# A hybrid decoder layer on one core: the delta rule's scan in one PSUM bank, and four edits beside it

## Time and profile before

| | us |
|---|---|
| median of 3 runs (lowest, highest) | 1223.63 (1221.22, 1224.39) |
| profiled execution, its own time | 1222.85 |
| its span, first to last instruction | 1221.1 |
| PE busy / PEld busy | 1151.6 / 936.6 |
| DVE / ACT / POOL busy | 801.5 / 558.4 / 483.8 |
| mean granted clock of PE | 0.991 |

### The profile page before, as it was taken

The page is one execution under the profiler, slowest core; times in us unless marked ns, Lnnn a source line. Parts: engine busy times, 40 slices in busy tenths (PEclk is TensorE's granted clock), DMA queues, the critical chain, the costliest instruction groups (busy, mean ns, idle before and its releaser), DMA issues.

```text
span 1221.1 us, 22297 instructions
## 1 busy us (share of the span) xinstructions
PE 1151.6 (94%) x9202; PEld 936.6 (77%) x9202; DVE 801.5 (66%) x1093; ACT 558.4 (46%) x1005; POOL 483.8 (40%) x420
## 2 busy tenths in 40 slices
PE   5999999889998989999998999999999999999996
PEld 4778879877777776767666778888888888888784
DVE  5798977457788888888874854333333333777974
ACT  6544233346554445454555654333333334446442
POOL 2476346212022021220213024554445554875972
PEclk9999999999999999999998999999999999999998
DMA  7345121400000000000105443222222221553561
GB/s 247 85 114 178 54 50 46 89 22 22 2 21 21 2 22 2 21 2 3 36 10 182 144 152 101 70 69 74 82 69 70 69 77 62 211 185 121 186 227 69
DMA packets 104076, 99.82 MB, mean 82 GB/s; under 512 B 15412, under 2 KB 89384, under 8 KB 103976
## 3 DMA queue, kind: packets, MB, share of 16 engines
q1 hardware_dynamic: 102536, 93.15, 25.1%
q10 hardware_dynamic: 1440, 5.24, 1.1%
HBM read 85.24 MB, written 13.11 MB: 81 GB/s over the span
## 4 chain that ended last, share of the span: by engine, by line
PE 69%; DVE 19%; ACT 5%; issue 4%; DMA 2%; SPq 1%; POOL 0%; DVEq 0%; ACTq 0%; POOLq 0%
PE psum L1694 25%; PE psum L1990 12%; PE psum L2531 6%; PE psum L1340 5%; PE psum L2571 4%; DVE arena L2414 3%; PE psum L1521 3%; PE psum L1587 3%; DVE pt_q L1237 2%; PE psum L1497 2%; PE psum L1537 1%; DVE arena L1218 1%; ACT pt_p L1017 1%; DVE ap_q L1866 1%; PE psum L1333 1%
## 5 line engine op out<-in xcount | busy, mean ns | idle before, releaser
L1694 PE MATMUL psum<-h_p,up_p 128*128 128x512 f32 x704 | 221.0, 390 | 0.7 <-DVE h_q L1683 0.5
L1694 PE MATMUL psum<-h_q,up_q 128*128 128x512 f32 x704 | 220.7, 389 | 0.0
L1760 POOL TENSOR_TENSOR up_q<-arena,up_p 128x1024 fp32r<-128x1024 f32 x44 | 105.9, 2406 | 212.3 <-ACT up_p L1756 212.3
L1811 DVE SCALAR_TENSOR_TENSOR arena<-psum,arena 128x1023 f32<-128x1023 f32 x44 | 56.4, 1283 | 196.1 <-ACT arena L1780 196.1
L1694 PEld LDWEIGHTS psum<-h_p,up_p 128*128 128x128 f32 x704 | 132.1, 188 | 28.9 <-DVE h_q L1683 1.0
L1694 PEld LDWEIGHTS psum<-h_q,up_q 128*128 128x128 f32 x704 | 132.2, 188 | 27.3
L1780 ACT ACTIVATE arena<-psum,arena 128x1024 f32<-128x1024 f32 x44 | 49.1, 1117 | 199.0 <-PE psum L1694 199.0
L1850 POOL TENSOR_TENSOR dn_q<-arena,dn_p 128x1024 fp32r<-128x1024 f32 x44 | 114.5, 2617 | 44.1 <-ACT dn_p L1846 44.1
L1866 DVE SCALAR_TENSOR_TENSOR ap_q<-ap_p,arena 128x512 fp32r<-128x512 f32 x44 | 108.9, 2499 | 29.3 <-ACT ap_p L1862 29.3
L1990 PE MATMUL psum<-dn_p,ap_p 128*128 128x512 f32 x352 | 110.7, 396 | 6.1 <-DVE ap_q L1866 6.1
L1340 PE MATMUL psum<-arena 64*64 64x64 f32 x3072 | 112.6, 223 | 3.5 <-DVE arena L1109 1.6
(11 more groups left out here) (299 smaller groups left out, 2327.0 us busy)
## 6 DMA issues: line engine op xcount, KB each, us to landing
arena<-in_ffn_w_up SPq DMA_DIRECT2D x44, 512.0 KB, 3.8
arena<-in_ffn_w_down SPq DMA_DIRECT2D x44, 512.0 KB, 3.5
arena<-in_w_in SPq DMA_DIRECT2D x20, 512.0 KB, 4.0
arena<-in_x SPq DMA_DIRECT2D x16, 512.0 KB, 5.0
qkv_mid<-arena ACTq DMA_DIRECT2D x9, 512.0 KB
...
```

The source lines that it names most:

```text
L1694: ins = pe.matmul(up_ps[j % 2][:, g, h * 512:(h + 1) * 512], w[:, k], x[:, k, h * 512:(h + 1) * 512], start=k == 0 and x is h2_p, stop=Tru ...
L1760: pool.tensor_tensor(up_q[up_slot(u)], up_st[up_slot(u)], up_p[up_slot(u)], ALU.subtract).then_inc(late("up_lo")[0], 1)
L1811: v.scalar_tensor_tensor(out=y[:, 1:S], in0=ps[:, 0:S - 1], scalar=tap(1, u), in1=y[:, 1:S], op0=ALU.mult, op1=ALU.add).then_inc(late("up_ ...
```

## The change

Five edits. (a) The scan: every step of both chunks uses bank 2. For a chunk the steps are now `B1`, `B3`, `C1`, `B2`: o is completed at once, ACT copies it out to `on` and squares it (two instructions for 64 rows each time, 16 times), and only then `B2` overwrites the place. `C1n` becomes one operation on `on` in SBUF rather than two that read PSUM. (b) `NT` uses bank 3 for every second step from the sixth on, with semaphores of its own, so that two turned blocks can stand at a time. (c) `ORDER` is another string throughout. (d) The down stage: from kk = 3 on DVE forms `dn_q`, just ahead of `ap_q`, and makes all residual additions; POOL has nothing left there. The two loads of norm gains ahead of the output stage are issued earlier and no longer one after the other. (e) The first two units are done by blocks of 256 tokens, the first after the transposes of tile 2.

```diff
 def gdn_scan(t):
-    return [("B1", t, 0), ("B2", t, 0), ("B1", t, 1), ("B2", t, 1), ("B3", t), ("C1", t), ("C1r", t), ("C1s", t), ("C1n", t), ("C2", t)]
+    return [(s, t, c) for c in range(2) for s in ("B1", "B3", "C1", "B2")] + [("C1r", t), ("C1s", t), ("C1n", t), ("C2", t)]
...
-    "gsgggiisgiisgssssssgstssgssssgsstssggsvvstsssgsssrvgvsgoisgosossggsstssgsvvtggvvstssgosssvvstggosssg"
...
+    "gsgggiisggiiisgsssgsssssgtsssgvsvssssggtssssggstssgvsrsgvsgosoogstssvggvvsvsgsstsstsggsosssvvvgstsgt"
...
+        nsa_nt = [s for s in MIX if s[0] == "NT"]
+        nsa_p3 = nsa_nt[5::2]
+        nsa_pt = [s for s in MIX if s[0] in ("Nq", "Nc2", "Nidx", "Nb", "No") or s in nsa_nt and s not in nsa_p3]
         def pt_use(step):
             return nsa_pt.index(step)
-        nsa_nt = [s for s in MIX if s[0] == "NT"]
-
-
-        nt_alt = [s for s in nsa_nt[-NT:] if nsa_pt[pt_use(s) - 1] in nsa_nt[-NT:]][::2]
-
-        def nt_bank(step):
-            return 4 if step in nt_alt else 6
+        def nt_at(step):
+            if step in nsa_p3:
+                return 3, sem("n_p3m"), sem("n_p3"), nsa_p3.index(step)
+            return 6, sem("n_ptm"), sem("n_pt"), pt_use(step)
+        def nt_turned(eng, step):
+            _, turned, _, u = nt_at(step)
+            eng.wait_ge(turned, u + 1)
...
+            def C1(t, c):
+                act.wait_ge(sem("b_o"), 2 * t + c + 1)
                 if t:
                     act.wait_ge(sem("c_ss"), t)
-                for rows, bank in O_AT:
-                    act.activation(flat(sq2)[rows], psum[rows, bank, 0:GDIM], ACT.Square).then_inc(sem("c_sq"), 1)
+                    act.wait_ge(sem("c_tp"), t)
+                rows = O_AT[c]
+                act.activation(flat(on)[rows], psum[rows, 2, 0:GDIM], ACT.Copy).then_inc(sem("c_oc"), 1)
+                act.activation(flat(sq2)[rows], psum[rows, 2, 0:GDIM], ACT.Square).then_inc(sem("c_sq"), 1)
...
+                v.tensor_tensor(flat(vn)[rows], psum[rows, 2, 0:GDIM], flat(uu[t % 2])[rows], ALU.add).then_inc(sem("b_vn"), 1)
...
-                for rows, bank in O_AT:
-                    v.tensor_tensor(on[rows], psum[rows, bank, 0:GDIM].rearrange("p (h d) -> p h d", h=GH), bc(rs2[rows], 2, HD), ALU.mult)\
-                        .then_inc(sem("c_on"), 1)
+                v.wait_ge(sem("c_oc"), 2 * t + 2)
+                v.tensor_tensor(on, on, bc(rs2, 2, HD), ALU.mult).then_inc(sem("c_on"), 1)
...
 def B2(t, c):
                 rows = (LO, HI)[c]
+                pe.wait_ge(sem("c_oc"), 2 * t + c + 1)
+                pe.wait_ge(sem("c_sq"), 2 * t + c + 1)
+                for h in range(GH):
+                    ins = pe.matmul(psum[(LO, HI)[h % 2], 2, h // 2 * CH:(h // 2 + 1) * CH], kdec[t % 2][rows, h], vn[rows, h],
+                                    start=h < 2, stop=True, skip_group_check=True)
+                ins.then_inc(sem("b_dm"), 1)
+
+            def B3(t, c):
+                rows = (LO, HI)[c]
+                pe.wait_ge(sem("g_QTc"), t + 1)
                 pe.wait_ge(sem("b_vn"), 2 * t + c + 1)
                 for h in range(GH):
-                    out_rows, bank = D_AT[c][h % 2]
-                    ins = pe.matmul(psum[out_rows, bank, h // 2 * CH:(h // 2 + 1) * CH], kdec[t % 2][rows, h], vn[rows, h],
-                                    start=h < 2, stop=True, skip_group_check=True)
-                ins.then_inc(sem("b_dm"), 1)
-
-            def B3(t):
-                pe.wait_ge(sem("g_QTc"), t + 1)
-                pe.wait_ge(sem("b_S"), 4 * t + 4)
-                for h in range(GH):
-                    for rows, (out_rows, bank) in zip((LO, HI), O_AT):
-                        ins = pe.matmul(psum[out_rows, bank, h * CH:(h + 1) * CH], QTc[t % 2][rows, h], vn[rows, h], start=False, stop=True,
-                                        skip_group_check=True)
+                    ins = pe.matmul(psum[O_AT[c], 2, h * CH:(h + 1) * CH], QTc[t % 2][rows, h], vn[rows, h], start=False, stop=True,
+                                    skip_group_check=True)
                 ins.then_inc(sem("b_o"), 1)
 
             def C2(t):
-                pe.wait_ge(sem("c_on"), 2 * t + 2)
+                pe.wait_ge(sem("c_on"), t + 1)
...
                 step = ("NT", t, kind, kv, b)
-                before = nsa_pt[pt_use(step) - 1] if pt_use(step) else None
-                if step in nt_alt:
-                    pe.wait_ge(sem("n_exp"), 2 * NH * NT)
-                if before in nsa_nt[-NT:] and nt_bank(before) != nt_bank(step):
-                    pe.wait_ge(sem("n_pt"), pt_use(step) - 1)
-                else:
-                    pt_free(step)
+                bank, turned, done, n = nt_at(step)
+                if step == nsa_p3[0]:
+                    pe.wait_ge(sem("kc_mul"), 4)
+                    pe.wait_ge(sem("vc_out"), 6)
+                if n:
+                    pe.wait_ge(done, n)
                 u = s_use(t, kind, GRP * kv)
                 pe.wait_ge(sem("n_exp"), u + GRP)
                 k0, _ = key_blocks(t, kind)
                 for g in range(GRP):
-                    ins = pe.transpose(psum[:, nt_bank(step), g * P:(g + 1) * P], probs(u + g)[:, (b - k0) * P:(b - k0 + 1) * P], ident)
-                ins.then_inc(sem("n_ptm"), 1)
+                    ins = pe.transpose(psum[:, bank, g * P:(g + 1) * P], probs(u + g)[:, (b - k0) * P:(b - k0 + 1) * P], ident)
+                ins.then_inc(turned, 1)
 
             def NV(t, kind, kv, b):
-                pe.wait_ge(sem("n_pt"), pt_use(("NT", t, kind, kv, b)) + 1)
+                _, _, done, u = nt_at(("NT", t, kind, kv, b))
+                pe.wait_ge(done, u + 1)
...
             sp.wait_ge(sem("n_sm"), 2 * NH * NT)
+            sp.dma_start(gpost_mix, a["norm_mix_post"][0].partition_broadcast(P)).then_inc(sem("gpost_in"), 16)
+            sp.dma_start(gffn, a["norm_ffn_pre"][0].partition_broadcast(P)).then_inc(sem("gpost_in"), 16)
             sp.wait_ge(sem("n_ptm"), pt_use(("No", NT - 1)) + 1)
             sp.wait_ge(sem("b_S"), 4 * NT)
             sp.wait_ge(sem("c_m"), 2 * NT)
             for t in range(3):
                 sp.dma_start(xr[t], x_d[0, t * P:(t + 1) * P, :]).then_inc(late(f"xr_in{t}")[0], 16)
-            sp.dma_start(gpost_mix, a["norm_mix_post"][0].partition_broadcast(P)).then_inc(sem("gpost_in"), 16)
-            sp.wait_ge(sem("gpost_in"), 16)
-            sp.dma_start(gffn, a["norm_ffn_pre"][0].partition_broadcast(P)).then_inc(sem("gpost_in"), 16)
...
-        def dn_split_lo(pool, kk):
-            pool.wait_ge(*late("dn_hi", kk + 1))
-            pool.tensor_tensor(dn_q[kk % 4], dn_st[kk % 4], dn_p[kk % 4], ALU.subtract).then_inc(late("dn_lo")[0], 1)
+        def dn_split_lo(eng, kk):
+            eng.wait_ge(*late("dn_hi", kk + 1))
+            eng.tensor_tensor(dn_q[kk % 4], dn_st[kk % 4], dn_p[kk % 4], ALU.subtract).then_inc(late("dn_lo")[0] if kk < 3 else sem("dn_lv"), 1)
+        def dn_ready(eng, kk):
+            eng.wait_ge(*late("dn_lo", kk + 1)) if kk < 3 else eng.wait_ge(sem("dn_lv"), kk - 2)
...
                 if kk >= 4:
-                    sp.wait_ge(*late("dn_lo", kk - 3))
+                    dn_ready(sp, kk - 4)
...
-            for kk in range(3, DN):
-                dn_split_lo(pool, kk)
-                if kk in (NF + 3, NF + 5):
-                    add(kk - NF - 3)
-            for t in range(HT, NT, 2):
-                add(t)
...
             for kk in range(2, DN):
                 if kk == NF + 2:
                     for t in range(HT):
                         finish(t)
+                if kk > 2:
+                    dn_split_lo(v, kk)
                 act_split_lo(v, kk)
 
-                if kk in (NF + 4, NF + 5):
-                    add(2 * (kk - NF - 4) + 1)
+                if NF + 4 <= kk < NF + 4 + HT:
+                    add(kk - NF - 4)
...
-            def unit(i, halves=(0, 1), ks=range(KD)):
+            def unit(i, blocks=((0, 512), (512, 1024))):
...
-                for k in ks:
+                for k in range(KD):
                     for w, x in ((p, h_p), (q, h_q)):
-                        for h in halves:
-                            ins = pe.matmul(cm_ps[i % 2][:, h * 512:(h + 1) * 512], w[:, k], x[:, k, h * 512:(h + 1) * 512],
+                        for c0, c1 in blocks:
+                            ins = pe.matmul(cm_ps[i % 2][:, c0:c1], w[:, k], x[:, k, c0:c1],
                                             start=k == 0 and x is h_p, stop=True, skip_group_check=True)
-                if 1 in halves:
+                if c1 == S:
...
-                if t >= NT // 2:
-                    pe.wait_ge(sem("h_lo"), NT // 2)
-                    if t == 6:
+                for i, b in {2: ((0, 0),), 4: ((1, 0),), 5: ((0, 1),), 6: ((1, 1),), 7: ((0, 2), (1, 2))}.get(t, ()):
+                    pe.wait_ge(sem("h_lo"), 2 * b + 2)
+                    if (i, b) == (1, 0):
                         pe.wait_ge(sem("pcol_ready"), 3)
```

(6 more changed lines are left out.)

72 lines of the change are left out of this document (28 added, 44 removed).

## The result

| | before | after |
|---|---|---|
| median of 4 runs each (lowest, highest), us | 1223.86 (1221.22, 1224.39) | 1206.23 (1204.77, 1206.69) |
| span of the profiled execution, us | 1221.1 | 1202.5 |
| PE / DVE / ACT / POOL busy, us | 1151.6 / 801.5 / 558.4 / 483.8 | 1143.9 / 765.5 / 559.7 / 365.9 |
| mean granted clock of PE | 0.991 | 0.989 |

The ratio is 0.9858, 95% interval 0.9841 to 0.9875: 17.6 us faster, where 9.5 were forecast. The time is inside the range and outside the likeliest case (1209 to 1218); it is that of rival 1.

The account below looks back on a forecast made before the run. PE was taken to bound the kernel (69% of the chain), edits elsewhere paying only where PE waits. Down -2.8, output -1.2, first -0.5, mixer -5.0 sum to -9.5: 1213.4 from 1222.85, 1214.1 us as median; range 1204 to 1227.

Parts of the forecast that it names:

- rival 1: Mixer: the order frees more, turning in pairs takes all 16.5 us of load waits; mixer some -14, time 1205; chance 0.17.
- Down stage, -2.8: Down stage: PE's first wait goes (-1.9), second shortens (-0.9), clock dip of some 2.4 us stays; bounds -5.2 and 0.
- First stage, -0.5: Front: last `h_q` about 0.5 us earlier, so DVE's chain from the rope tables gains 0.5; bounds -1.5 and +1.5.
- Rival 3: First stage: PE's longer idle time near 74 us drops the clock, costing up to 2.4 us: 1216.5; chance 0.08.
- (i): Mixer: second place for turned probabilities removes PE's 18 waits for `pt_q`, -7.4 us; bounds 0 and -16.5.
- (ii): Mixer: `C1n` as 8 operations instead of 16 saves DVE 4.4 us; a third taken, -1.4; bounds 0 and -4.4.
- (iv): Mixer: `B2` waits for copy and square, about 1.1 us per chunk, mostly hidden: +1; bounds 0 and +17.6.
- rival 4: Mixer: slower, `B2` behind ACT's copy and square costs PE about 2 us per exposed chunk; ten give 1233; chance 0.20.
- (iii): Mixer: ACT gains 16 copies, 7.7 us of work on an engine with free time: +0.8; bounds 0 and +7.7.
- (v) the end, +2: Mixer's end: fewer steps ahead of the last `C2`, a new copy of 0.48, output product at half clock; bounds 0 and +4.
- The rest of the new order: Mixer: remaining effect of the new order, not priceable from rows, taken as nought with 8 us to either side.
- Rival 2: Mixer stands still, waits for `pt_q` move to `NV`; only -4.5 is left, 1219.1 us; chance 0.17.

Follow-up runs that it names:

- b_down: Kernel before with only the down stage's second parts and residual additions moved from POOL to DVE, gain loads left as they were: 1218.66 us, ratio 0.9957.
- b_first: Kernel before with only the first units of products done in blocks of two tiles: 1221.67 us, ratio 0.9994.
- b_b3seq: Kernel before with `B3`'s two loops exchanged, six products of the lower rows, then six of the upper, instead of by turns: 1226.69 us, ratio 1.0023.
- b_scan: Kernel before with only the scan in bank 2, its copies and one `C1n`; old order except the scan's own steps, placed anew: 1232.94 us, ratio 1.0078.
- a_oldorder: Changed kernel with the old written order, only the scan's own steps placed anew, second bank in use: 1220.84 us, ratio 0.9987 to the kernel before.
- a_split: Changed kernel with 36 of 37 side-by-side pairs of `NT` steps taken apart in the order: 1214.64 us, ratio 0.9929 to the kernel before.

## Why the prediction was right or wrong

**Down stage, -2.8.** Mechanism right, size short: -3.8 in the changed kernel, -5.4 alone (-4.6 by the medians). `ap_q` has its 0.684 in the median and `dn_q` 1.225 on DVE, both as priced; the first wait is gone, the second is 3.16 (3.3 forecast). The mis-sized term is the dip of the clock, "I leave in place", which measured 0.8 us less in the changed kernel and 2.4 less in b_down, where it did not come; the bound of -5.2 had allowed for that. Why the clock fell in four of the five traces with this wait and not in the fifth stays open.

**Output stage, -1.2.** Mechanism right in the traces, size not measurable in the medians. DVE's wait for the gain went, and with it PE's wait of 1.2 us ahead of the first turned tile, as said. The stage is 3.1 us shorter, since the new order also took the last `NV` and the wait ahead of the last `No` out of it, a term that the prediction does not have.

**First stage, -0.5.** Not shown (b_first), and the place was wrong: the step "PE's idle time there grows to some 2.7 us" put it at unit 6, near 74 us, where PE did not wait at all. It came ahead of unit 2, since ScalarE's copy of unit 0 was late. Rival 3's fall of the clock came with it (pairs at 1.05 us), but there DVE sets the pace and it cost nothing.

**Mixer, -5.0.** Measured -10.8, and the sum of the terms hid two steps that failed, in opposite directions.
- *(i) second bank, -7.4:* -8.6 under the old order by the traces, 7.5 at most by the medians. The size is right. The mechanism is right only in part: the waits ahead of the transposes went, but most of that idle time came back at other steps (2.3 us less in all), and 6.3 us of the gain is busy time. That the sizes agree is in part luck.
- *(ii) to (iv), the scan, together +0.4:* +9.2 in the trace (434.4 - 425.2), +9.7 in the medians. The step that failed is one that the prediction does not have: it costed what `B3` waits for and not how its products follow each other on PE. The lost alternation costs 3 us by the medians, 4.6 by the traces (b_b3seq). `B2` waits for ACT by 1.5 us, near the +1 of (iv), in the changed kernel 0.6, so rival 4's mechanism is out. By busy and idle time b_scan's 9.2 are 7.2 in `B3`, 0.6 in other work and 1.4 in waits; how the 7.2 divide between alternation (5.0 of busy time in b_b3seq) and smaller groups is not shown, nor is the part of my placing of the steps. The moved work has the sizes priced in (ii) and (iii): in the mixer DVE is busy 4.4 us less in b_scan, ACT 5.5 more. But the -1.4 that (ii) expected of it is not seen; it was not tried alone.
- *(v) the end, +2:* the last wait grew by 1.6 us (2.8 to 4.4), but not for the reasons given. 1.8 us of it was POOL beside `C1n`, which now has two SBUF operands and, by the new order, runs beside the subtraction of `wo_q`: with the same `C1n` and the old order (b_scan, a_oldorder) all eight take 0.55 us. The prediction had measured that very effect in the down stage, and did not carry it over to this operation. The Trainium skill (SBUF — State Buffer, "Who interferes with whom") says that a DVE instruction with two SBUF inputs contends with a GpSimd instruction that reads SBUF; here the trace agrees, 2.37 against 0.56 us. That the old form, which read PSUM, would have been spared was not tried.
- *"The rest of the new order I can't price from rows; I take it as nought":* -11.4 in the mixer, -14.1 with the output stage, 14.6 by the medians. This is the step that decided the size. Taking 36 pairs of turned blocks apart costs 9.2 in the mixer and 8.4 by the medians (a_split), 5.7 in PE's busy time and 3.5 in waits. The rest of what the order gave stays open. That is rival 1, "turning in pairs", close to its time (1205 forecast, 1206.2 measured), but that the time agrees is in part luck: it had -14 for the mixer and -4.5 for all else, where -10.8 and -7.5 were measured. Its working went by the 16.5 us of waits of the earlier trace rows, where more than half of what pairs gave was busy time, which no row of waits holds.

Together: -8.6 + 9.2 - 11.4 = -10.8 for the mixer, so the total came inside the range although two terms were off by 9 and by 11 us: they cancelled in part, and that is luck. Rival 2 was half right in its mechanism: `NV`'s waits rose from 2.7 to 6.1 us.
